# A one-core hybrid decoder step: gate/up weight pieces of 256 half rows, and the gate half of a block finished first

## The reference

```
gu = xb @ w_gu[e] + b_gu[e]                  # w_gu[e]: 1024 x 2048
gate, up = gu[:, :D_FF], gu[:, D_FF:]
gate = jnp.minimum(gate, SWIGLU_LIMIT)
up = jnp.clip(up, -SWIGLU_LIMIT, SWIGLU_LIMIT)
hmid = (up + 1.0) * gate * jax.nn.sigmoid(SWIGLU_ALPHA * gate)
y = hmid @ w_down[e] + b_down[e]             # w_down[e]: 1024 x 1024
```

## Time and profile before

| | |
|---|---|
| median of three runs | 1336.25 us (1333.88 to 1337.16) |
| profiled execution | 1336.53 us |
| its span | 1334.8 us, 19255 instructions |
| granted clock of TensorE, mean | 0.986 |
| PE busy | 1286.9 us (96%) |
| DVE busy | 473.7 us (35%) |
| HBM read, written | 443.88 MB, 6.26 MB |
| DMA packets | 103987: under 512 B 11697, under 2 KB 20987, under 8 KB 71078 |

### The profile page before, as it was taken

How to read it: one execution, slowest core, us unless ns; L and a number is a source line. 1 busy time by engine, 2 the same in 40 slices (tenths; PEclk the granted TensorE clock), 3 DMA queues, 4 the chain that set the end, 5 groups by cost and what they waited for, 6 DMA issues and landing times.

```text
span 1334.8 us, 19255 instructions
## 1 busy us (share of the span) xinstructions
PE 1286.9 (96%) x7213; PEld 564.0 (42%) x7213; DVE 473.7 (35%) x991; ACT 200.6 (15%) x337; POOL 65.6 (5%) x146
## 2 busy tenths in 40 slices
PE   6999999998989999999999999999999999999996
PEld 5777766665433333333333333333333333333332
DVE  2083668154535233322223332222232322222244
ACT  2223521312520000000000000000000000000002
POOL 3002010101210000000000000000000000000000
PEclk9999899998989999999999999999999999999999
DMA  9343126328689999999999999999999999999994
GB/s 296 126 144 128 51 74 187 139 72 281 245 358 356 418 418 418 419 417 417 417 417 419 418 419 418 418 418 416 417 417 418 419 418 418 419 418 416 417 416 188
DMA packets 103987, 450.58 MB, mean 338 GB/s; under 512 B 11697, under 2 KB 20987, under 8 KB 71078
## 3 DMA queue, kind: packets, MB, share of 16 engines
q1 hardware_dynamic: 98948, 446.18, 83.5%
q10 hardware_dynamic: 5002, 3.89, 1.1%
HBM read 443.88 MB, written 6.26 MB: 337 GB/s over the span
## 4 chain that ended last, share of the span: by engine, by line
PE 46%; DMA 12%; SPq 11%; issue 1%; DVE 1%; ACT 0%
PE ps L994 21%; PE ps L1020 12%; DMA ring<-in_w_gu 10%; SPq L366 6%; PE ps L967 5%; SPq L361 4%; PE ps L946 3%; DMA ring<-in_w_down 2%; PE ps L960 1%; PE ps L954 1%; PE ps L975 1%; PE ps L1013 1%; PE ps L984 1%; DVE x_tok L1801 0%; DVE x_tok L1743 0%
## 5 line engine op out<-in xcount | busy, mean ns | idle before, releaser
L994 PE MATMUL ps<-ring,proj 128*64 128x512 f32 x2024 | 465.5, 599 | 6.6 <-DMA ring<-in_w_gu 6.6
L1020 PE MATMUL ps<-ring,proj 128*64 128x512 f32 x1024 | 245.7, 601 | 1.8 <-DMA ring<-in_w_down 1.4
L994 PEld LDWEIGHTS ps<-ring,proj 128*64 128x64 f32 x2024 | 137.3, 137 | 254.1 <-issue 202.8
L1718 DVE TENSOR_SCALAR proj<-ps 128x512 f32<-128x512 f32 x32 | 22.1, 691 | 396.9 <-PE ps L994 395.9
L1743 DVE TENSOR_TENSOR x_tok<-x_tok,ps 96x512 f32<-96x512 f32 x192 | 122.6, 679 | 98.4 <-PE ps L967 98.4
L1020 PEld LDWEIGHTS ps<-ring,proj 128*64 128x64 f32 x1024 | 64.9, 136 | 153.0 <-issue 146.3
L967 PE MATMUL ps<-proj 64*96 64x512 f32 x384 | 105.3, 627 | 0.6 <-DVE proj L1732 0.6
L599 PE MATMUL ps<-feat,ring 128*128 128x288 f32 x384 | 99.4, 411 | 0.0
L567 PE MATMUL ps<-feat,ring 128*128 128x288 f32 x384 | 95.6, 412 | 2.2 <-DVEq L1331 2.2
L567 PEld LDWEIGHTS ps<-feat,ring 128*128 128x128 f32 x384 | 73.8, 193 | 23.3 <-DVE feat L1330 2.4
L599 PEld LDWEIGHTS ps<-feat,ring 128*128 128x128 f32 x384 | 71.2, 191 | 21.8 <-issue 3.1
(11 more groups left out here) (358 smaller groups left out, 898.8 us busy)
## 6 DMA issues: line engine op xcount, KB each, us to landing
ring<-in_w_gu SPq DMA_DIRECT2D x253, 1024.0 KB, 19.7
ring<-in_w_down SPq DMA_DIRECT2D x128, 1024.0 KB, 22.5
ring<-in_w_in SPq DMA_DIRECT2D x12, 2048.0 KB, 9.2
out<-states SPq DMA_DIRECT2D x1, 2048.0 KB, 8.7
ring<-in_w_oa SPq DMA_DIRECT2D x1, 2048.0 KB, 8.9
ring<-in_w_ob SPq DMA_DIRECT2D x1, 2048.0 KB, 10.9
ring<-in_w_out SPq DMA_DIRECT2D x1, 2048.0 KB, 8.2
out<-states ACTq DMA_DIRECT2D x1, 2048.0 KB, 9.5
```

The lines of the kernel that those rows point to most:

```text
L994: last = mm(bank(j // 2)[64 * (j % 2):64 * (j % 2) + 64, :], xgT[:, k % 4, k // 4, :], w[:, 512 * j:512 * j + 512], start=False, stop=k == ...
L1020: last = mm(bank(4)[64 * j:64 * j + 64, :], hidT[:, k % 4, 64 * (k // 4):64 * (k // 4) + 64], ring[:, KT + k // 2, n:n + 512], start=False ...
L1718: ts(hid_g, bank(0), SWIGLU_LIMIT, None, ALU.min).then_inc(sg["gate_clipped"], 1)
```

## The change

A gate/up piece now holds 256 rows of one half: pieces 0 to 3 are the gate columns (0 to 1023) of rows 0 to 255, 256 to 511, 512 to 767 and 768 to 1023, and pieces 4 to 7 the up columns of the same rows. A partition gets row p and row 128+p of the piece, 1024 f32 each. PE makes the same four products for a piece, but of two groups of 128 rows into one bank, so that bank 0 is complete after the fourth piece and bank 1 after the eighth. DVE waits for the fourth piece, clips the gate, then waits for the eighth, and goes on as before.

```diff
+            def gu_piece(e, k):
+                rows, cols = slice(256 * (k % 4), 256 * (k % 4) + 256), slice(D * (k // 4), D * (k // 4) + D)
+                src = w_gu[0, e, rows, cols] if isinstance(e, int) else \
+                    w_gu[0][bass.ds(e, 1), rows, cols].rearrange("a p n -> (a p) n")
+                return src.rearrange("(a p) n -> p a n", a=2)
+
             def gu_load(e, k):
-                src = w_gu[0, e, 128 * k:128 * k + 128, :] if isinstance(e, int) else \
-                    w_gu[0][bass.ds(e, 1), 128 * k:128 * k + 128, :].rearrange("a p n -> (a p) n")
-                sp.dma_start(ring[:, k, :], src).then_inc(w_arrived[k], 16)
+                sp.dma_start(ring[:, k, :].rearrange("p (a n) -> p a n", a=2), gu_piece(e, k)).then_inc(w_arrived[k], 16)
...
             for k in range(len(extra)):
-                sp.dma_start(extra[k], w_gu[0, 1, 128 * k:128 * k + 128, :]).then_inc(sg[f"wx_in{k}"], 16)
+                sp.dma_start(extra[k].rearrange("p (a n) -> p a n", a=2), gu_piece(1, k)).then_inc(sg[f"wx_in{k}"], 16)
...
-                    for j in range(4):
-                        last = mm(bank(j // 2)[64 * (j % 2):64 * (j % 2) + 64, :], xgT[:, k % 4, k // 4, :],
-                                  w[:, 512 * j:512 * j + 512], start=False, stop=k == KT - 1)
+                    for a in range(2):
+                        c = 2 * (k % 4) + a
+                        for j in range(2):
+                            last = mm(bank(k // 4)[64 * j:64 * j + 64, :], xgT[:, c % 4, c // 4, :],
+                                      w[:, D * a + 512 * j:D * a + 512 * j + 512], start=False, stop=c == KT - 1)
                     last.then_inc(sg["gu_used"], 1)
...
             def hidden(b, more=True):
+                dve.wait_ge(sg["gu_used"], GU0 + KT * b + KT // 2)
+                ts(hid_g, bank(0), SWIGLU_LIMIT, None, ALU.min).then_inc(sg["gate_clipped"], 1)
                 dve.wait_ge(sg["gu_used"], GU0 + KT * b + KT)
-                ts(hid_g, bank(0), SWIGLU_LIMIT, None, ALU.min).then_inc(sg["gate_clipped"], 1)
                 ts(hid_u, bank(1), SWIGLU_LIMIT, -SWIGLU_LIMIT, ALU.min, ALU.max).then_inc(sg["up_clipped"], 1)
```

## The result

The changed kernel takes 1354.67 us (median of 4, 1353.49 to 1356.27), the kernel before 1336.7 us in the same comparison. The ratio is 1.0136, 95% interval [1.0121, 1.0151]: slower by 18.0 us. The forecast was 1351.8 us. The profiled execution took 1353.49 us with a span of 1351.6 us, 16.8 us more than before.

The account below looks back on a forecast made before the run. The prediction took the saturated DMA queue to set the time: its start, all pieces behind it, plus the tail. Slower pieces (16.1 us) less the early clip (0.7 us) add 15.4 us, giving 1351.8 us, range 1346 to 1358.

Parts of the forecast that it names:

- What bounds the kernel: Saturated DMA queue from 408 us needs 30.13 us a block, PE 29.20; from about 899 us transfers set the time.
- end of PE's lead: PE's 15.3 us lead over the transfers gone after 10 blocks: first gate/up wait near 710 us, not 899.
- The price of a piece: In the saturated queue, 4 KB runs cost each of 234 gate/up pieces 0.069 us more: 16.1 us.
- The stride: Gate/up rows read 8 KB apart: no extra cost, argued from a w_in transfer's strided 2 KB runs at 408 GB/s.
- The upper bound: Slowest strided rows in the trace, the state load with 512 B runs at 288 GB/s: 3.64 us a gate/up piece.
- The early clip: DVE's gate clip moved ahead shortens PE's 1.66 us wait between blocks 0 and 1: -0.7 us, nothing worthwhile elsewhere.
- the tail: What follows the last awaited down piece of the last block but one: 29.1 us, expected unchanged.
- a term of +0.4 us: About six earlier gate/up pieces would also pay if the queue's idle part at 400 to 408 us were closed.
- The sum: Whole kernel: 16.1 - 0.7 = 15.4 us slower, giving 1351.8 us, 1.2% more.
- The order of products and the banks: On PE, four products in a row into one bank instead of two and two: costs nothing.
- The rule of small packets: Skill page's fixed cost of about 3 cycles per DMA packet: 0.029 us a piece, 6.8 us in all; not used.
- Rival C: SP's issue of transfers becomes the bound: 49 us a block, some 570 us more over 30 blocks; chance 1%.

Follow-up runs that it names:

- e1: Changed kernel with gate/up pieces again 128 whole rows (8 KB runs), new product order and early gate clip kept: 1336.56 us, ratio 1.0001 against the kernel before.
- e7: Changed kernel (early gate clip) loading only half of each down piece from block 1 on: 1323.1 us, ratio 0.9894 against the kernel before.
- e8: Changed kernel with the late gate clip, loading only half of each down piece from block 1 on: 1324.31 us, ratio 0.9902 against the kernel before.
- e2: Changed kernel with each gate/up piece read from one run of memory, cut into 4 KB packets without stride: 1353.14 us, ratio 1.0121 against the kernel before.
- e3: Changed kernel with each gate/up piece read from one run of memory, cut into 2 KB packets, four per partition: 1389.35 us, ratio 1.0396 against the kernel before.
- e4: Changed kernel with the gate clip back behind the eighth piece, new transfers kept: 1355.83 us, ratio 1.0145 against the kernel before.

## Why the prediction was right

- **What bounds the kernel.** Right. e1 moves the time by changing transfers alone; e7 and e8 take the queue off the path, and the 12.6 us that transfers were reckoned to cost from 899 us on are gone (13.0 in e8, which like the kernel before has the late clip). The forecast's end of PE's lead was near 710 us; the first long wait is at 723.
- **The price of a piece.** Right in mechanism, slightly small in size: 0.069 us was used, the blocks give 2.560 - 2.487 = 0.073, so 234 x 0.073 = 17.1 us instead of 16.1. Of the two values that the prediction had, the one from the block's period (0.071) was nearer. The other came from two windows of 7 and 16 us, whose rates are given to 1 GB/s, and 1 GB/s is 0.006 us a piece.
- **The stride.** Priced at nothing: shown by e2. The row it was argued from was no support for it, however, so that this step was right by luck. The 408 GB/s of a w_in transfer come from 2.5 us in the middle of one transfer; 12 us of 2 KB runs in the saturated queue move 387 GB/s (e3). The row stands 5% too high, more than the 2.9% that were to be priced. The upper bound (288 GB/s, the state) was taken for strided rows; with the price that e3 shows, its short runs alone would account for it.
- **The early clip.** The wait between blocks 0 and 1 fell by 0.67 us as said. Whether the -0.7 us arrived at the end is not shown. The profiled loss ahead of the tail is 16.85 us. The transfers make 17.1 with 0.073 us a piece and 17.3 with the periods not rounded ((61.44 - 60.26)/16 = 0.0738), which would leave -0.25 to -0.4 for the clip. But the prediction also named a term of +0.4 us, for six pieces more, if the idle time of the queue before 408 us were closed, and it nearly is. With it the sum is 17.3 + 0.4 - 0.7 = 17.0, and the clip may have brought all of its 0.7. DMA in 380:420 of the kernel before, of e1 (old pieces, early clip), of the changed kernel and of e4 (new pieces, late clip):

```profile
q1 hardware_dynamic: 1897, 13.73, 88.8%
...
q1 hardware_dynamic: 1921, 13.83, 90.0%
...
q1 hardware_dynamic: 3639, 14.06, 96.2%
...
q1 hardware_dynamic: 3661, 14.14, 96.5%
```

  The queue is idle for about 4.5, 4.0, 1.5 and 1.4 us of these 40. So it is the slower pieces that fill the idle time, with either clip. A finer reading is not possible: the part ahead of the experts ends at another time in each execution (SP's issue of these pieces begins at 378.17 us in e4 and at 380.62 in e1), by more than the clip is worth.
- **The sum.** 15.4 us were forecast; the profiled execution shows 17.0 (1353.49 - 1336.53) and the medians 18.0. Of the 1.6 us between forecast and profiled execution, 1.0 to 1.2 is the price of a piece; the rest is the closed idle time or the clip, which can't be told apart. The last 1 us between profile and medians is within the spread of the executions: the profiled one was the fastest of its four (1353.49 to 1356.27).
- **The order of products and the banks.** Nothing that can be told, as said (e1; 599 ns again).
- **The rule of small packets.** Behind the 9.1 and 9.4 ns a packet of e3: the Trainium skill, DMA: Bandwidth & Descriptors, section Why small descriptors are slow (HBM only), has about 3 cycles a packet, which as an estimate from that page would be 1.2% from 8 KB to 4 KB; the blocks show 2.9%. That each packet costs a fixed time holds here, the size given for it does not, and no run shows where in the chip the time is spent.
- **Rival C.** Not so, and worth a look, because the chain seems to say the opposite. In the changed kernel it gives 24% of the span to SP's issues of gate/up pieces, and one issue takes 2149 ns in the median, against 841 before:

```profile
L365 SPq DMA_DIRECT2D ring<-in_w_gu x253: 363/2149/3372, 322.0 to 1293.3; - x127
DMA to landing us min/median/max: 5.8/18.3/19.1
```

  That the time follows the packets (e2, e3) does not settle it, since an issue could cost time for each packet too. Two other things do. A piece lands 18.3 us after its issue, and the queue moves one in 2.56 us, so some seven pieces lie ahead of it: SP is ahead of the engines and not behind them. And the down pieces, whose transfers are alike in all three kernels, take 1159 ns to issue before, 2149 in the changed kernel and 1110 in e3:

```profile
L370 SPq DMA_DIRECT2D ring<-in_w_down x128: 367/2149/4918, 325.4 to 1324.7; - x128
...
L370 SPq DMA_DIRECT2D ring<-in_w_down x128: 368/1110/2658, 333.5 to 1360.7; - x128
```

  So the time of an issue is mostly waiting for room in the queue. The median from issue to landing of gate/up pieces fell from 19.7 to 18.3 us, and to 14.3 us in e3.

## What to carry to other kernels

When a DMA queue is saturated for most of a kernel, the length of the contiguous run that one partition gets has a price: count the runs behind the start of saturation and price each (here 9 ns on each engine, 2.9% between 8 KB and 4 KB, 18 us of this kernel). A layout that finishes one half of the work sooner is worth only what some engine really waited for, here 0.7 us once and 0.02 us a block; look for that wait before cutting rows in two. The same sum read backwards finds gains: giving each partition two adjacent rows, and reordering the small operand to match, made this kernel 8.5 us faster than it was.

## What the runs showed of the hardware

- A run costs a fixed time beside its bytes in a saturated queue: 2.487, 2.560 and 2.710 us for 1 MiB in runs of 8, 4 and 2 KB. Carried on to no runs at all this leaves, as an estimate, 2.487 - 8 x 0.0092 = 2.413 us, or 434 GB/s.
- A stride of 8 KB between runs of 4 KB costs nothing that can be seen: 410 GB/s with and without it.
- Weight loads of a 128x128 transpose that reads every second f32 take 209 ns instead of 140. With four of them in a block, the block took 0.1 us more (29.30 against 29.20).
- A queue with more packets per byte has fewer bytes in flight: from issue to landing a gate/up piece took 19.7, 18.3 and 14.3 us in the median at 8, 4 and 2 KB, while each piece took longer to move.
- The time of an issue on SP says nothing of its own cost in a full queue: the same down transfer took 1159, 2149 and 1110 ns in the median, by what else was queued.
